# Expert loop of a mixture-of-experts block: 1024-wide weight units, full-height bias products, down bias added once, 1024-wide gating, four split slots

## What is computed

```python
gu = xb @ w_gu + b_gu                                  # 1024 -> 2048
x_glu, x_lin = gu[..., :D_EXPERT], gu[..., D_EXPERT:]
x_glu = jnp.minimum(x_glu, SWIGLU_LIMIT)               # limit 7
x_lin = jnp.clip(x_lin, -SWIGLU_LIMIT, SWIGLU_LIMIT)
act = x_glu * jax.nn.sigmoid(SWIGLU_ALPHA * x_glu) * (x_lin + 1.0)
return act @ w_dn + b_dn                               # 1024 -> 1024
```

## Time and profile before

| | |
|---|---|
| median of 3 runs | 1649.65 us (1648.27 to 1652.71) |
| span of the profiled execution | 1646.3 us |
| granted TensorE clock, mean | 0.971 |
| TensorE busy | 93% of the span |
| VectorE busy | 78% |
| ScalarE busy | 60% |
| GpSimd busy | 34% |
| bytes moved by DMA | 458 MB |

### The profile page before, as it was taken

The page is one execution under the profiler, slowest core; times in us unless marked ns, Lnnn a source line. Parts: engine busy times, 40 slices in busy tenths (PEclk is TensorE's granted clock), DMA queues, the critical chain, the costliest instruction groups (busy, mean ns, idle before and its releaser), DMA issues.

```text
span 1646.3 us, 21271 instructions
## 1 busy us (share of the span) xinstructions
PE 1532.2 (93%) x6812; PEld 1184.5 (72%) x6812; DVE 1291.6 (78%) x1165; ACT 988.9 (60%) x749; POOL 554.8 (34%) x446
## 2 busy tenths in 40 slices
PE   6989989499999999999999999999999999999960
PEld 5877877477777777777777777777777777777740
DVE  5444453578888888888888888888888888888867
ACT  4333232466676666667666677676666766666731
POOL 0000000403444444444444444443444444434412
PEclk9999989699999999999999999999999999999985
DMA  8221221579999999999999999999999999999915
GB/s 289 77 77 65 90 81 64 163 249 334 330 335 332 343 330 338 315 337 342 327 337 328 334 338 334 338 331 339 337 338 328 330 332 330 334 329 340 336 67 230
DMA packets 226809, 458.06 MB, mean 278 GB/s; under 512 B 13296, under 2 KB 13312, under 8 KB 225568
## 3 DMA queue, kind: packets, MB, share of 16 engines
q1 hardware_dynamic: 215136, 436.23, 75.1%
q0 software_dynamic: 9984, 18.79, 3.1%
q10 hardware_dynamic: 1664, 2.71, 0.5%
HBM read 454.01 MB, written 20.97 MB: 289 GB/s over the span
## 4 chain that ended last, share of the span: by engine, by line
PE 78%; DMA 10%; DVE 4%; issue 4%; ACT 2%; POOLq 2%; POOL 1%; ACTq 0%; SPq 0%; DVEq 0%
PE ps L1190 23%; PE ps L1192 21%; PE ps L1191 21%; DMA y_rows<-y,idx_scatter 5%; PE ps L1466 4%; DMA xg<-h_rows,idx_gather 4%; PE ps L1443 2%; PE ps L1452 1%; POOL tab L477 1%; POOLq L493 1%; ACT y L718 1%; DMA x<-in_x 1%; PE ps L1311 1%; PE ps L1433 1%; PE ps L1280 1%
## 5 line engine op out<-in xcount | busy, mean ns | idle before, releaser
L800 DVE TENSOR_TENSOR wlo<-raw,whi 128x2048 fp32r<-128x2048 f32 x274 | 625.3, 2290 | 191.8 <-ACT whi L575 191.7
L575 ACT ACTIVATE whi<-raw 128x2048 fp32r<-128x2048 f32 x274 | 525.7, 1919 | 293.8 <-PE ps L1192 151.2
L1190 PE MATMUL ps<-whi,xT_hi 128*128 128x512 f32 x1024 | 416.0, 406 | 5.5 <-DVE xT_lo L1058 5.5
L1192 PE MATMUL ps<-whi,xT_lo 128*128 128x512 f32 x1024 | 404.0, 394 | 0.0
L1191 PE MATMUL ps<-wlo,xT_hi 128*128 128x512 f32 x1024 | 403.2, 394 | 0.0
L1190 PEld LDWEIGHTS ps<-whi,xT_hi 128*128 128x128 f32 x1024 | 193.1, 189 | 67.4 <-issue 29.4
L1192 PEld LDWEIGHTS ps<-whi,xT_lo 128*128 128x128 f32 x1024 | 193.1, 189 | 43.2
L1191 PEld LDWEIGHTS ps<-wlo,xT_hi 128*128 128x128 f32 x1024 | 193.5, 189 | 38.5
L1190 PE MATMUL ps<-whi,actT_hi 128*128 128x512 f32 x512 | 208.2, 407 | 4.6 <-DVE actT_lo L1065 4.6
L469 POOL TENSOR_SCALAR has<-slots,pair 128x128 fp32r<-128x128 f32 x128 | 170.1, 1340 | 115.9 <-issue 115.9
L1191 PE MATMUL ps<-wlo,actT_hi 128*128 128x512 f32 x512 | 201.9, 394 | 0.0
(11 more groups left out here) (195 smaller groups left out, 1781.4 us busy)
## 6 DMA issues: line engine op xcount, KB each, us to landing
raw<-in_w_gate_up SPq DMA_DIRECT2D x130, 1024.0 KB, 7.0
raw<-in_w_down SPq DMA_DIRECT2D x126, 1024.0 KB, 6.2
raw_a<-in_w_gate_up SPq DMA_DIRECT2D x63, 1024.0 KB, 5.4
raw_b<-in_w_gate_up SPq DMA_DIRECT2D x63, 1024.0 KB, 6.4
raw<-in_w_in SPq DMA_DIRECT2D x14, 1024.0 KB, 5.2
picked<-y_rows SPq DMA_DIRECT2D x8, 1024.0 KB, 12.7
raw<-in_w_out SPq DMA_DIRECT2D x4, 1024.0 KB, 5.0
x<-in_x SPq DMA_DIRECT2D x4, 512.0 KB, 8.1
```

Source lines behind the costliest of these rows:

```text
L575: nc.scalar.activation(whi[:, n % SPLIT, :], raw_slot(slot_of(n)), ACT.Copy).then_inc(hi_done, 1)
L800: nc.vector.tensor_tensor(wlo[:, n % SPLIT, :], raw_slot(slot_of(n)), whi[:, n % SPLIT, :].bitcast(F32), ALU.subtract).then_inc(lo_done, 1)
L1190: mm(out_ap, x_hi_ap, w_hi_ap, start=start, stop=False)
L1192: return mm(out_ap, x_lo_ap, w_hi_ap, start=False, stop=stop)
```

## The change

Units keep their size but now hold two pieces of 1024 columns (`KM` = 2, `MW` = 1024), so a row of a transfer has 4 KB. Each unit feeds two banks. From the experts' units on there are four split slots (`whi3`, `wlo3` are new). The bias product has all 128 rows (rows 64 to 127 are cleared once) and comes first in its bank; the two gate-and-up halves of the columns each get their pair of biases ahead of their units. `sel_dn` is gone, and the down bias leaves the loop: after it, the gates of all experts are transposed and multiplied with `b_down` in eight products, and VectorE adds the result to the residual. The gating works 1024 wide: Sigmoid straight from PSUM, multiply, one clamp with the +1 folded into the bias, and one operation for minimum and multiply (`GATED_MAX` is the value of the clamped branch). Each engine's loop now has the units 30 to 41.

```diff
+SPLIT_E = 4
+KM = 2
+MW = 1024
...
+def units_before_split(n):
+    return n - SPLIT + 1 if n < U_MOE + SPLIT else n - SPLIT_E + 1
...
-    wgu_v = w_gate_up[0].rearrange("e (k p) (g c) -> p e g k c", p=P, c=UW)
-    wdn_v = w_down[0].rearrange("e (k p) (g c) -> p e g k c", p=P, c=UW)
+    wgu_v = w_gate_up[0].rearrange("e (k p) (g c) -> p e g k c", p=P, c=MW)
+    wdn_v = w_down[0].rearrange("e (k p) c -> p e k c", p=P)
...
                 pl.wait_ge(used, i * U_E + (U_LOOP + U_GU))
                 select(sel_gu, i + 2).then_inc(sel_gu_s, 1)
-                pl.wait_ge(used, i * U_E + (U_LOOP + U_E))
-                select(sel_dn, i + 1).then_inc(sel_dn_s, 1)
                 pl.wait_ge(y_s, i + 2)
                 scatter(expert_rows(i), scattered)
...
+            def sigmoid(e, i=0):
+                act_e.wait_ge(used, i * U_E + (U_MOE + U_GU // 2 if e == 0 else U_LOOP + (e - 1) * U_E + U_GU // 2))
+                if e > 0:
+                    act_e.wait_ge(act_s, i + e)
+                nc.scalar.activation(sig[:, :], ps[:, 0:2, :].rearrange("p b t -> p (b t)"), ACT.Sigmoid,
+                                     scale=ALPHA).then_inc(sig_s, 1)
...
             sigmoid(0)
             hi(26)
             hi(27)
+            act_e.wait_ge(sq, 2 * NC)
+            act_e.dma_start(gain_row[:, :], norm_final_g.rearrange("(o d) -> o d", o=1).to_broadcast([P, D])).then_inc(fin_g_in, 16)
+            hi(28)
+            hi(29)
             tokens_hi(1)
-            hi(28)
-            sigmoid(1)
             with act_e.Fori(0, E - 1) as i:
-                hi(29, i)
                 hi(30, i)
+                hi(31, i)
                 features_hi(0, i)
                 copy_table(2, i)
-                for n in (31, 32, 33):
-                    hi(n, i)
-                sigmoid(2, i)
-                for n in (34, 35, 36):
+                hi(32, i)
+                hi(33, i)
+                sigmoid(1, i)
+                for n in (34, 35, 36, 37):
                     hi(n, i)
                 tokens_hi(2, i)
-                hi(37, i)
-                sigmoid(3, i)
-                for n in (38, 39, 40):
+                for n in (38, 39, 40, 41):
                     hi(n, i)
                 gated_rows(i, i + 1, i * U_E + (U_LOOP + U_E))
+            act_e.wait_ge(x_lo, E + 1)
+            for r in (0, E, 2 * E):
+                act_e.dma_start(bdn_raw[r:r + E, :], b_down[0]).then_inc(bdn_in, 16)
             features_hi(E - 1)
...
+            def gate_glu(e, i=0):
+                v.wait_ge(sig_s, i + (e + 1))
+                nc.vector.tensor_tensor(sig[:, :], ps[:, 0:2, :].rearrange("p b t -> p (b t)"), sig[:, :], ALU.mult).then_inc(glu_s, 1)
+            def clamp_lin(e, i=0):
+                v.wait_ge(used, i * U_E + (U_MOE + U_GU if e == 0 else U_LOOP + (e - 1) * U_E + U_GU))
+                nc.vector.tensor_scalar(lin[:, :], ps[:, 2:4, :].rearrange("p b t -> p (b t)"), LIMIT + 1.0, 1.0 - LIMIT,
+                                        ALU.min, ALU.max).then_inc(lin_s, 1)
+            def activated(e, i=0):
+                v.wait_ge(glu_s, i + (e + 1))
+                v.wait_ge(lin_s, i + (e + 1))
+                nc.vector.scalar_tensor_tensor(out=act[:, :], in0=sig[:, :], scalar=GATED_MAX, in1=lin[:, :], op0=ALU.min,
+                                               op1=ALU.mult).then_inc(act_s, 1)
...
+            gate_glu(0)
+            for n in (27, 28, 29):
+                lo(n)
+            clamp_lin(0)
+            tokens_lo(1)
             activated(0)
...
             with v.Fori(0, E - 1) as i:
-                lo(29, i)
                 lo(30, i)
+                lo(31, i)
                 features_lo(0, i)
-                lo(31, i)
                 lo(32, i)
-                gate(2, i * U_E + (U_LOOP + 4), i)
                 lo(33, i)
-                activated(2, i)
-                for n in (34, 35, 36):
-                    lo(n, i)
-                gate(3, i * U_E + (U_LOOP + 8), i)
+                lo(34, i)
+                gate_glu(1, i)
+                lo(35, i)
+                lo(36, i)
+                lo(37, i)
+                clamp_lin(1, i)
+                lo(38, i)
                 tokens_lo(2, i)
-                lo(37, i)
-                activated(3, i)
-                for n in (38, 39, 40):
-                    lo(n, i)
+                lo(39, i)
+                activated(1, i)
+                lo(40, i)
+                lo(41, i)
...
+            def add_bias(bank, col):
+                mm(ps[:, bank, :], sel_gu[:, :], bias[:, col:col + UW], start=True, stop=False)
+            def unit_matmuls(n, i, k0, bank, x_hi_t, x_lo_t, started):
+                unit_wait(n, i)
+                for k in range(KM):
+                    kk = k0 + k
+                    for half in range(2):
+                        w_hi_ap, w_lo_ap = unit_part(n, 2 * k + half)
+                        last = three(ps[:, bank + half, :], x_hi_t[:, kk, :], x_lo_t[:, kk, :], w_hi_ap, w_lo_ap,
+                                     kk == 0 and not started, kk == KD - 1)
+                last.then_inc(used, 1)
...
-                for q in range(4):
-                    if e > 0 and q % 2 == 0:
-                        pe.wait_ge(lin_s, i * 2 + (2 * e + q // 2 - 1))
-                    if q == 1 and e > 0:
+                if e > 0:
+                    pe.wait_ge(glu_s, i + e)
+                for half in range(2):
+                    add_bias(half, half * UW)
+                for u in range(U_GU):
+                    if u == 2 and e > 0:
                         features(e - 1, i)
-                        pe.wait_ge(lin_s, i * 2 + 2 * e)
+                        pe.wait_ge(lin_s, i + e)
                         table(e + 1, i)
-                    if q == 3:
+                    if u == 4:
                         pe.wait_ge(tab_raw, i + (e + 2))
-                    half_matrix(n0 + 2 * q, i, q, sel_gu, GU_COLS[q] * UW, xT_hi, xT_lo)
+                        for half in range(2):
+                            add_bias(2 + half, D + half * UW)
+                    unit_matmuls(n0 + u, i, KM * (u % 4), 2 * (u // 4), xT_hi, xT_lo, True)
```

More of the change, by code:

```diff
@@ L516, in _ @@
             select(sel_gu, 1).then_inc(sel_gu_s, 1)
-            select(sel_dn, 0).then_inc(sel_dn_s, 1)
             pl.sem_inc(y_free, 1)
@@ L1489, in down @@
                 pe.wait_ge(y_s, i + (e + 1))
-                for q in range(2):
-                    half_matrix(n0 + 2 * q, i, 4 + q, sel_dn, 2 * D + q * UW, actT_hi, actT_lo)
+                for u in range(U_DN):
+                    unit_matmuls(n0 + u, i, KM * u, 4, actT_hi, actT_lo, False)
             table(0)
@@ L1505, in _ @@
             features(E - 1)
-            down(U_ALL - U_DN, E - 1)
+            pe.wait_ge(gate4_s, 1)
+            pe.wait_ge(glu_s, E)
+            for c in range(NC):
+                last = nc.tensor.transpose(ps[:, 0, c * P:(c + 1) * P], gate4[:, c, :, :].rearrange("p g e -> p (g e)"), ident)
+            last.then_inc(gate_tr, 1)
+            down(U_ALL - U_DN, E - 1)
+            pe.wait_ge(gateT_lo, 1)
+            pe.wait_ge(bdn_s, 1)
+            pe.wait_ge(bdn_zero, 1)
+            for c in range(NC):
+                if c == NC - 1:
+                    pe.wait_ge(xb_s, 1)
+                for half in range(2):
+                    last = mm(ps[:, GB_BANK[c] + half, :], gateT[:, c * P:(c + 1) * P], bdn[:, half * UW:(half + 1) * UW],
+                              start=True, stop=True)
+                last.then_inc(gb_s, 1)
+            pe.wait_ge(xb_s, NC)
             for r in range(RAW):
@@ L1514, in _, with whole_matrix @@
                     with pe.If(i < total):
[L1515 to L1517 removed]
+                        def whole_matrix(q, x_t, biased):
+                            for u in range(4 * q, 4 * q + 4):
                                 pe.wait_ge(v_full[u % RAW], i * (16 * U_E // RAW) + 16 * (u // RAW + 1))
[L1519 to L1522 removed]
+                                for k in range(KM):
+                                    kk = KM * (u % 4) + k
+                                    for half in range(2):
+                                        col = k * MW + half * UW
+                                        last = mm(ps[:, 2 * q + half, :], x_t[:, kk, :], raw[:, u % RAW, col:col + UW],
+                                                  start=(kk == 0 and not biased), stop=(kk == KD - 1))
                                 last.then_inc(v_free, 1)
```

248 lines of the change are left out of this document (121 added, 127 removed).

## The result

The changed kernel takes **1700.98 us** (median of 4 runs, 1696.78 to 1702.61) against 1649.12 of the kernel before beside it: ratio 1.031, 95% interval 1.029 to 1.034. It is 52 us slower; 1599 was forecast, and the range ended at 1668. The profiled execution spans 1700.0 us.

The account below looks back on a forecast made before the run. TensorE sets the pace, with the gather's chain a close second bound. From the 1646.3 us span, 52.5 off for 37.5 us passes and 1.5 added ahead of the loop give 1595.3, plus 3.35 to the median: 1599; range 1566 to 1668.

Parts of the forecast that it names:

- TensorE's gain: In the loop: two bias products leave and four become ordinary, so TensorE's own pass falls from 39.25 to 36.4 us.
- the 0.63 us: On TensorE: cost of one 64-row bias product in the kernel before, 0.52 where transposes follow; 3.56 us a pass.
- the pass of 37.5 us: In the loop: tokens start at 25.5 us, plus 12.0 to the next zero; 30 passes gain 52.5 us.
- `lo(41)` from 2.19 to 4.48: On VectorE: the scatter's cast ends behind `lo(41)` at 4.48, so its issue at 5.34 leads `lo(30)` by 0.04 us.
- the winning side: On GpSimd: the scatter's issue starts before `lo(30)` and ends at about 6.4 instead of 8.3 us; chance 0.45.
- the gather misses its slot: Rival: `lo(30)` starts before the scatter's issue, the gather's issue falls into a `lo`, landing near 27.5; 1665 us, chance 0.22.
- the rival's price: In the loop: a missed slot makes passes of 39.6 to 39.8 us, total 1665; chance 0.22.
- L477 (now L515) just ahead of a `lo`: On GpSimd: it gets through ahead of the `lo` at 15.0, the cast ends at 17.4, the gather is issued at 18.2.
- Ahead of the loop: Before the loop: later tokens and half clock cost 5.4 us, cheaper bias products save 3.9; together +1.5 us.
- Rows of 4 KB: On DMA: costed at nothing to the weights; a rival had them hold up gather and scatter, over 1800 us, chance 0.08.
- VectorE's sum of 33.6 us of 36.4: In the loop: 12 units of 2.29 and five operations of 1.22 us do not make VectorE the bound.
- The landing of 7.2 us: In the loop: the gather, issued at 18.2, lands 7.2 us later, taken above the 6.8 median for longer landings.

Follow-up runs that it names:

- version 3: Changed kernel, with VectorE gating first and beginning `lo(34)` only once GpSimd has issued the gather; 1582.41 us, ratio 0.958 to the kernel before.
- Run 5: Kernel before, with only its six bias products a pass made full height (all 128 rows); 1594.09 us, ratio 0.967.
- run 6: version 3 with its four bias products cut back to 64 rows; 1591.97 us, ratio 0.965 to the kernel before.
- run 4: Changed kernel with eight unused products on TensorE ahead of its wait for the gather; 1656.86 us, ratio 1.005 to the kernel before.
- Run 12: version 3 with the order ahead of the loop mended, `lo(30)` held as well, both holds released by a memset behind the issue; 1603.1 us, ratio 0.972.
- run 10: Kernel of Run 5 with the first gating trio put behind the `lo` that follows it; 1683.69 us, ratio 1.022 to the kernel before.
- run 7: version 3 with each expert unit loaded by two DMAs of 512 columns, in 2 KB pieces; 1598.22 us, ratio 0.970 to the kernel before.
- run 1: Changed kernel with the gather's table and issue moved ahead of the wait for the scatter on GpSimd; 1688.15 us, ratio 1.023 to the kernel before.
- run 8: version 3 with `lo(30)` also held until the scatter's issue, by an increment sent behind the scatter; 1749.22 us, ratio 1.061 to the kernel before.
- run 2: Kernel before, with the gather's table and issue moved ahead of the wait for the scatter on GpSimd; 1643.46 us, ratio 0.9965.

## Why the prediction was wrong

**TensorE's gain: right.** The bias products run at plain intervals, and in version 3 a pass less its wait is 36.2 to 36.4 us against the 36.4 of the working. Run 5 shows 54 us of gain from height alone. What I priced wrongly is the unit: of the 0.63 us, 0.40 are the price of two switches of height, and would have been half for products in pairs (run 6). That changed nothing here.

**The term that failed is the pass of 37.5 us.** It was 41.0, and 30 x 3.5 = 105 us is all of the miss of 102. One step of the working missed the slot, another priced the miss too low.

**The first failed step: `lo(41)` from 2.19 to 4.48.** I counted the race of the scatter's issue with `lo(30)` in hundredths: the cast free at 4.48, the issue at 5.34, `lo(30)` at 5.38. `lo(30)` came at 814.32 - 808.95 = 5.37 as worked out. But I started `lo(41)` from its `hi` alone and did not ask whether VectorE was free: it was still in `lo(40)`, which began at 0.56, and both ended at 5.04. The issue came at 5.95. It was no toss-up but lost by 0.58 us, and I gave the winning side 0.45.

**The rival "the gather misses its slot" is what happened, nearly to the row.** Counted from zero it had L513 through at 17.3 (the `lo` it waited for ended at 17.3), the gather's issue at 18.9 (18.8), inside the `lo` of 18.3 to 20.6 (18.2 to 20.5), landing near 27.5 (transposes at 27.2). Its chance should have been well above 0.22. The traces of the two kernels and the twelve runs hold 864 issues of gathers and scatters from 400 us on. The 571 that began 0.07 to 0.78 us behind the start of a `lo` lasted 2.45 to 3.17 us, and every one ended 0.93 to 0.97 us behind the end of that `lo`; the 293 others lasted 0.98 to 1.32. The Trainium skill, "SBUF — State Buffer", section "SBUF: two separate sides", has the same rule: the port pair that VectorE and GpSimd share belongs to whoever starts first, for the whole instruction. The traces agree.

**The second failed step: the rival's price, a pass of 39.6 to 39.8.** It took 41.0 on average, since I charged the half clock once, in the prologue (2.2 us), and not behind the wait of every pass. From the transposes of one pass to the `y` of the next are 15.6 us instead of the 14.0 that version 3 shows; run 4 gives the clock 44 us. 1665 + 44 = 1709, against 1701 measured. The range ended at 1668, too low for its own rival, for that reason.

**The winning side was perhaps no win by itself.** Run 12 has the scatter's issue at 1.09 us, and the gather still leaves only 0.35 earlier, as the next `lo` catches L515. I had put L477 (now L515) just ahead of a `lo`; I was building on a second tie behind the first. A kernel in which only the scatter's issue is freed was not run. With the gather's issue alone freed (run 3) the scatter's still took 2.6 us and the loss was gone, and run 10 shows the edit that spoils it: the gating behind a `lo` instead of ahead of it. The change made that move as its units run one ahead of before (the fourth slot), so that the gating falls one `lo` later; I listed the order and costed it at nothing; run 3 puts 119 us on it and run 10 shows 90.

**Other steps.** Ahead of the loop: a stall of 6.48 us where I had 2.8 + 3.2 = 6.0, right. From the start to the first of the 30 passes it took 3.9 us more, and behind the last 2.3 less: together 1.6 where I had 1.5 and 0, so the sum is right partly by luck. Rows of 4 KB: costed at nothing, and no harm (run 7). VectorE's sum of 33.6 us of 36.4 as no bound: right for the changed kernel, but it left no room for holds (run 12). The landing of 7.2 us: the median from issue to landing was 8.6, of which 2.6 was the issue; behind its end that is 6.0, and the forecast had 7.2 - 1.07 = 6.1.

## What to carry to other kernels

Where two engines share a resource that a long operation holds to its end, list for each short operation on the critical chain which long one begins next to it, and start every long one from the later of its data and its own engine's queue; a lead below half a microsecond in such a list is a risk to be priced on both sides, with the clock's fall behind every wait that results. A faster bounding engine doesn't keep a tuned order: look at what the reordering puts in front of the second chain. And a hold is cheap (0.4 us of VectorE in a pass, and 119 us off the kernel), but it must be released when the guarded instruction has begun for certain, and it should guard one place only if the held engine has no slack for more.

## What the runs showed of the hardware

- The issue of an indirect DMA on GpSimd, 1.06 us by itself, waits for a VectorE operation with two inputs in SBUF that began before it: 571 issues in 14 traces ended 0.93 to 0.97 us behind that operation's end. A lag of 0.07 us was enough, and with a lead of 0.01 the issue was free (runs 1, 3 and 8).
- GpSimd idled 3.9 to 6.7 us at a `drain` with a scatter of its own under way, until 0.30 us behind the scatter's landing in 60 passes, and 0.35 us without (runs 1 and 2).
- A semaphore increment behind an indirect DMA on GpSimd let a `lo` begin 0.08 to 0.10 us before the issue itself (run 8), or 0.00 to 0.01 after its start (run 3): it does not tell that the issue is done.
- 64-row products among 128-row ones cost 0.39 us for the pair of switches, whether one or two products stand between them (run 6).
- After a wait of about 3 us TensorE ran at 0.50 of its clock for about 3 us, and eight dummy products ahead of the wait took 44 us off the kernel (run 4).
- The same gather landed in a median of 5.0 us (run 5), 5.9 (run 3), 6.8 (before) and 7.2 (run 12) after its issue began, and in the loop, from 400 us on, no `lo` held any of these issues. Runs 3 and 7 show a part of 1 us for the way the weights are fetched (one DMA with rows of 4 KB, or two with 2 KB); the rest is open.
